# A differential-attention stage: the second map's weight moves from VectorE into PE's transposes, and row maxima are written negated

## The chip, the cores and the metric

The kernel runs on one core of a Trainium2 chip, in one launch. Its time is the device time of that core in microseconds (us); lower is better. The engines are PE (TensorE, matrix products), DVE (VectorE), ACT (ScalarE), POOL (GpSimd) and SP (SyncE, which here only issues DMAs). They run side by side and meet at semaphores; each works through its own instructions in order.

## The reference, cut to what matters

The reference is one step of a two-layer decoder over a prompt of 512 tokens and eight sample sequences of one new token each. Layer 1 is gated linear attention, layer 2 is differential attention with a linear position bias, and both end in a mixture of experts. Only differential attention bears on the change. For the prompt:

```python
bias = jnp.where(dist >= 0, -slopes[:, None, None] * dist, -jnp.inf)
p1 = jax.nn.softmax(jnp.einsum('bqhd,bkhd->bhqk', qf[..., :DH_B], k1) + bias, axis=-1)
p2 = jax.nn.softmax(jnp.einsum('bqhd,bkhd->bhqk', qf[..., DH_B:], k2) + bias, axis=-1)
return jnp.einsum('bhqk,bkhv->bqhv', p1 - lam * p2, vf)
```

There are 8 heads; queries come in 4 blocks of 128; causality lets block i see (i + 1) x 128 keys. For the samples, each of the 8 sequences attends with the same two-map rule over 2048 cached keys and values, kept in 16 pages of 128 positions (512 KB for keys and 512 KB for values, each), and its own new one.

## The kernel before, in words

The stage `stage_attention` does both jobs in one loop of eight passes. Pass b computes head b of the prompt and the scores of sample sequence b; the value products of sequence b-1 run in it too. Passes 0, 1 and 7 are written out, 2 to 6 are a loop on the chip. Every engine has its own order, written out by hand; there is no planner.

A pass has four blocks, i = 0 to 3 (a unit u = 4b + i is one query block of one head).

VectorE, in block i (`body` of the vector engine): the sums of key pages 4i and 4i+1 (`sum_page`, L2108: a reduce of a product of 128x1024 to 16 numbers per partition); `weigh` of the block before (L2065 to L2071); `keep` (L2075, the finished output of an earlier block out of PSUM); the sum of page 4i+2; `multiply` (L2098: key page 4i+4 by the query row); the sum of page 4i+3; and `unit` (bias onto the scores, L2084; row maxima, L2088; their sign, L2090). Behind block 3 come the sum of the new key's product, the softmax of the sample scores (L2140 to L2160) with `weigh` of block 3 inside it, and `fold`.

`weigh` makes lm = -lam * l1 / l2 from the two row sums l1 and l2 (ScalarE's exponentials accumulate them), and L2071 adds lm times the second map to the first, over (i + 1) x 128 columns. `keep` scales by 1 / l1 at the end.

GpSimd multiplies the three key pages in four that VectorE doesn't (L1894, 128x1024), into two buffers. Product n may start when the sum of product n-2 is done.

ScalarE, per unit: `c_copy` (L2017, the transposed map out of PSUM) for the block before, then the two exponentials (L2037) once VectorE has posted `nb_ok` at L2090. In a pass it also copies keys and queries of the next head, writes a finished sample row (`row_out`) and takes the exponential of the sample scores (L2048).

PE, in block i: the scores of the unit (L1976); values of pages 4i and 4i+1 of the sequence before (L1940); `finish` of the block before, that is the transposes of the weighed map (L1911, one per 128 columns, waiting for `c_ok` of L2071) and its product with the values (L1916); values of pages 4i+2 and 4i+3. Behind block 3: the small products of the sample softmax (L1959 to L1963), then `finish` of block 3.

SP issues the page loads: keys into a ring of eight page buffers, freed by the sums; values into a ring of four, freed by PE's value products; once a pass the query row of the sequence, broadcast to all partitions (L1866).

In `stage_queries`, which runs ahead, VectorE copies lam out of PSUM (L1746) into a column of `small`.

Of the kernel before, what the change touches and what calls it, by code (L numbers as in the profile page):

```python
# [9 lines left out]
ALU = mybir.AluOpType  # L10
ACT = mybir.ActivationFunctionType
AX = mybir.AxisListType


P = 128
D = 1024
# [1605 lines left out]
def stage_queries(nc, ctx, m, a, ahead):  # L1622

    sem = lambda n: ctx.enter_context(m_semaphore(nc, f"q_{n}"))
# [14 lines left out]
    m.pt = m.small[0:1, 128:128 + NS * PAGES].bitcast(I32)  # L1639
    t0, t1, pt_in = sem("t0"), sem("t1"), sem("pt_in")  # L1640
    m.coef = m.small[:, 33:34]
    sh_mm, sh_cp = sem("sh_mm"), sem("sh_cp")
    shares = m.R[:, 7168:7680]
    qs = m.R[0:NS, 5120:6144]
# [6 lines left out]
    with nc.Block() as block:  # L1651
# [75 lines left out]
        @block.vector  # L1727
        def _(v):
            v.wait_ge(t0, 3)
            for h in range(HB):  # L1730
                nc.vector.tensor_scalar(m.bt[:, 0:PAGES, 2 * h:2 * h + 2], nd.unsqueeze(2).to_broadcast([P, PAGES, 2]),
                                        2.0 ** (-8.0 * (h + 1) / HB), None, ALU.mult)
            for c in range(2):
                v.wait_ge(sh_mm, c + 1)
                wait(v, smm, c)
                nc.vector.tensor_copy(shares, m.ps[5][:, :]).then_inc(sh_cp, 1)
            v.wait_ge(l_in, 64)
            nc.vector.tensor_tensor(lprod, lrow[:, 0:2 * DHB], lrow[:, 2 * DHB:4 * DHB], ALU.mult)
            v.drain()
            nc.vector.tensor_reduce(out=lsum, in_=lprod.rearrange("p (a b) -> p a b", b=DHB), axis=AX.X, op=ALU.add).then_inc(l_sum, 1)  # L1740
            v.wait_ge(l_exp, 1)
            nc.vector.tensor_tensor(lam1, lsum[:, 0:1], lsum[:, 1:2], ALU.subtract)
            v.drain()
            nc.vector.tensor_scalar(lam1, lam1, LAM_INIT, None, ALU.add).then_inc(l_row, 1)
            v.wait_ge(l_mm, 1)
            nc.vector.tensor_copy(m.lam, m.ps[4][:, 0:1])  # L1746
            v.wait_ge(tab3, 1)
            nc.vector.tensor_reduce(out=odd1, in_=odd8, axis=AX.X, op=ALU.add)
            v.drain()

            nc.vector.tensor_tensor(m.coef, odd1, m.lam, ALU.mult)
            v.drain()
            nc.vector.tensor_tensor(m.coef, m.coef, odd1, ALU.add)
            v.drain()
            nc.vector.tensor_scalar(m.coef, m.coef, -1.0, 1.0, ALU.mult, ALU.add)


def stage_attention(nc, ctx, m, a):
# [6 lines left out]
    sem = lambda n: ctx.enter_context(m_semaphore(nc, f"at_{n}"))  # L1765
    kr_ok, k_tr, kt_ok, sc_mm, sb_ok, nb_ok, p_ok, c_ok, c_tr, c_cp, o_mm, o_ev = (sem(n) for n in
        ("kr_ok", "k_tr", "kt_ok", "sc_mm", "sb_ok", "nb_ok", "p_ok", "c_ok", "c_tr", "c_cp", "o_mm", "o_ev"))
# [3 lines left out]
    v_in = [sem(f"v_in{u}") for u in range(2)]  # L1771
    q_in, kn_in, vn_in, o_out, os_in, z_ok = (sem(n) for n in
        ("q_in", "kn_in", "vn_in", "o_out", "os_in", "z_ok"))
    dp_ok, pp_ok = sem("dp_ok"), sem("pp_ok")
    ks_ok, mx_ok, mx_tr, mr_ok, mb_mm, sh_ok, e_ok, l_ok, l_mm, l_ev, pv_mm, om_ok, or_mm, or_ev = (sem(n) for n in
        ("ks_ok", "mx_ok", "mx_tr", "mr_ok", "mb_mm", "sh_ok", "e_ok", "l_ok", "l_mm", "l_ev", "pv_mm", "om_ok",
         "or_mm", "or_ev"))
    NQ = SEQ // P
# [9 lines left out]
    mx = [m.small[:, 40 + 2 * u:42 + 2 * u] for u in range(2)]  # L1788
    ls = [m.small[:, 44 + 2 * u:46 + 2 * u] for u in range(2)]
    r1 = [m.small[:, 48 + i:49 + i] for i in range(NQ)]  # L1790
    lm = m.small[:, 52:53]

    kp = [m.W[:, u * D:(u + 1) * D] for u in range(4)] + [m.lnr[:, 0, :], m.lnr[:, 1, :],
                                                        m.kk[:, NTT - 1, :], m.vv[:, NTT - 1, :]]
    vp = [m.W[:, (4 + u) * D:(5 + u) * D] for u in range(4)]
    xtf = m.xt[:, :, :].rearrange("p k t -> p (k t)")
    qb, kn = xtf[:, 0:D], xtf[:, D:2 * D]

    v_prod, g_prod = xtf[:, 2 * D:3 * D], [xtf[:, 3 * D:4 * D], m.v[:, NTT - 1, :]]
# [25 lines left out]
    with nc.Block() as block:  # L1825
# [72 lines left out]
        def _(pe):  # L1898
# [6 lines left out]

            def finish(u, i, h):

                pe.wait_ge(c_ok, u + 1)
                wait(pe, c_cp, u)
                for j in range(i + 1):  # L1910
                    last = nc.tensor.transpose(CT_B[:, j * P:(j + 1) * P], SP[i % 2][0][:, j * P:(j + 1) * P], m.ident[:, :])  # L1911
                last.then_inc(c_tr, 1)
                pe.wait_ge(c_cp, u + 1)
                wait(pe, o_ev, u)
                for j in range(i + 1):
                    last = nc.tensor.matmul(O_B[:, (i % 2) * DVB:(i % 2 + 1) * DVB], ct[i % 2][:, j * P:(j + 1) * P],  # L1916
                                            m.vv[:, j, bass.ds(h * DVB, DVB)], start=(j == 0), stop=(j == i))
                last.then_inc(o_mm, 1)
# [80 lines left out]
        @block.scalar  # L1999
        def _(s):  # L2000
            def stage(h):

                wait(s, k_tr, h)
                nc.scalar.copy(khr, m.kk[:, 0:NQ, bass.ds(h * P, P)]).then_inc(kr_ok, 1)

            def q_copy(h):
                wait(s, sc_mm, NQ * h)
                nc.scalar.copy(qh, m.qt[:, bass.ds(h, 1), :].rearrange("p a t -> p (a t)"))

            def k_copy(h):  # L2010
                s.wait_ge(k_tr, h + 1)
                nc.scalar.copy(kth, KT_B[:, :]).then_inc(kt_ok, 1)

            def c_copy(u, i):
                s.wait_ge(c_tr, u + 1)
                wait(s, o_mm, u - 1)
                nc.scalar.copy(ct[i % 2][:, 0:(i + 1) * P], CT_B[:, 0:(i + 1) * P]).then_inc(c_cp, 1)  # L2017

            def row_out(b):
                s.wait_ge(or_mm, b + 1)  # L2020
                wait(s, o_out, 16 * b)
                for n in range(2):
                    last = nc.scalar.copy(orow[:, n * 512:(n + 1) * 512], SC_B[n][0:1, :])
                last.then_inc(or_ev, 1)
                s.wait_ge(or_ev, b + 1)
                s.dma_start(m.osD[bass.ds(b, 1), :], orow).then_inc(o_out, 16)

            def body(b):
                st = isinstance(b, int)
                for i in range(NQ):  # L2030
                    u = NQ * b + i
                    if i:
                        c_copy(u - 1, i - 1)
                    s.wait_ge(nb_ok, u + 1)
                    for j in range(2):
                        x = SP[i % 2][j][:, 0:(i + 1) * P]
                        last = nc.scalar.activation(x, x, ACT.Exp, bias=mx[i % 2][:, j:j + 1], accum_out=ls[i % 2][:, j:j + 1])  # L2037
                    last.then_inc(p_ok, 1)
                    if i == 1 and not (st and b == HB - 1):
                        stage(b + 1)  # L2040
                    if i == NQ - 1 and not (st and b == HB - 1):
                        q_copy(b + 1)
                        k_copy(b + 1)
                    if i == 1 and not (st and b < 2):
                        row_out(b - 2)
                s.wait_ge(sh_ok, b + 1)
                wait(s, pv_mm, VG * b)
                nc.scalar.activation(PR[:, :, 0:C], S, ACT.Exp).then_inc(e_ok, 1)  # L2048
                c_copy(NQ * b + NQ - 1, NQ - 1)
            s.wait_ge(z_ok, 2)  # L2050
            stage(0)
            q_copy(0)
            k_copy(0)
            seqs(s, body)
            row_out(NS - 2)
            row_out(NS - 1)

        @block.vector
        def _(v):
            V = nc.vector  # L2060
            def weigh(u, i):

                v.wait_ge(p_ok, u + 1)
                p1, p2 = (SP[i % 2][j][:, 0:(i + 1) * P] for j in range(2))
                V.reciprocal(r1[i], ls[i % 2][:, 1:2])  # L2065
                V.tensor_scalar(lm, ls[i % 2][:, 0:1], m.lam, -1.0, ALU.mult, ALU.mult)
                v.drain()
                V.tensor_tensor(lm, lm, r1[i], ALU.mult)
                v.drain()
                V.reciprocal(r1[i], ls[i % 2][:, 0:1])  # L2070
                V.scalar_tensor_tensor(out=p1, in0=p2, scalar=lm, in1=p1, op0=ALU.mult, op1=ALU.add).then_inc(c_ok, 1)  # L2071

            def keep(u, i, h):
                v.wait_ge(o_mm, u + 1)
# [3 lines left out]
            def unit(b, i):  # L2078
                st = isinstance(b, int)
                u, w = NQ * b + i, (i + 1) * P  # L2080
                v.wait_ge(sc_mm, u + 1)
                wait(v, c_tr, u - 1)
                for j in range(2):
                    V.scalar_tensor_tensor(out=SP[i % 2][j][:, 0:w], in0=m.dist[:, SEQ - w:SEQ], scalar=m.slope[:, bass.ds(b, 1)],  # L2084
                                           in1=SC_B[j][:, 0:w], op0=ALU.mult, op1=ALU.add).then_inc(sb_ok, 1)
                v.drain()
                for j in range(2):
                    V.tensor_reduce(out=mx[i % 2][:, j:j + 1], in_=SP[i % 2][j][:, 0:w], axis=AX.X, op=ALU.max)  # L2088
                v.drain()
                V.tensor_scalar(mx[i % 2], mx[i % 2], -1.0, None, ALU.mult).then_inc(nb_ok, 1)  # L2090

            def multiply(b, j):

# [138 lines left out]
```

## Time and profile before

| | us |
|---|---|
| median of 3 runs | 2310.33 (2310.22 to 2314.02) |
| the profiled execution | 2309.59 |
| its span, first to last instruction | 2307.8 |
| PE busy in the span | 1646.7 (71%) |
| DVE busy | 905.0 (39%) |
| POOL busy | 388.8 (17%) |
| ACT busy | 373.9 (16%) |
| mean granted TensorE clock | 0.824 of 2.4 GHz |

The attention stage runs from about 1211 to 1720 us of the span. The shares of the table are means over stages with quite different limits, so the stage is to be read by itself. A matmul is listed with PE and its weight load with PEld. A row of the timeline gives start, duration, engine, line, operation, output<-input with their shapes, a count where neighbours were merged and, in brackets, the engine's idle time before and what ended it. On DVE an instruction's record overlaps the next one's by some 0.1 us.

### The profile page before, as it was taken

To read this page: it belongs to the slowest core of one execution; us is meant where nothing else is said; L and a number is where in the kernel's file an instruction comes from. 1 tells how busy PE (TensorE), PEld (TensorE's weight loads), DVE (VectorE), ACT (ScalarE), POOL (GpSimd) and SP (SyncE) were. 2 spreads that over 40 slices of the span, in tenths; PEclk is the share of its full clock that TensorE was granted. 3 is DMA by queue.
4 is the path that set the end of the run, shared out by engine and by line. 5 is a ranking of instruction groups with operands and counts; after the bars stand their busy time and mean duration, and the time that the engine had idled before them with its cause. 6 is when DMAs were issued, how large, how long until landed. Compare 5 with 4: busy or idle time off the path is not lost. (4 is left out here: it accounts for less than half of the span.)

```text
span 2307.8 us, 21696 instructions
## 1 busy us (share of the span) xinstructions
PE 1646.7 (71%) x6774; PEld 689.3 (30%) x6775; DVE 905.0 (39%) x1432; ACT 373.9 (16%) x723; POOL 388.8 (17%) x279
## 2 busy tenths in 40 slices
PE   3999967682789996489792555555557649989970
PEld 1443334231333332044331122222213323333320
DVE  1000154745100000720208999999946430000007
ACT  0001121111221222210011111111112101222222
POOL 0000000010100000300105555545510100000004
PEclk7999976695899998689895677777788759999995
DMA  7562513406698997842306777778752258999973
GB/s 277 193 249 82 213 73 115 163 0 248 267 428 348 391 428 312 325 136 77 110 1 239 282 277 290 288 268 299 282 189 104 72 203 347 376 428 428 428 330 111
DMA packets 109276, 558.27 MB, mean 242 GB/s; under 512 B 13438, under 2 KB 22399, under 8 KB 87692
## 3 DMA queue, kind: packets, MB, share of 16 engines
q1 hardware_dynamic: 95306, 508.41, 56.4%
q0 software_dynamic: 7904, 28.45, 3.3%
q10 hardware_dynamic: 5992, 20.48, 2.2%
q8 instruction: 41, 0.67, 0.1%
q14 instruction: 33, 0.26, 0.0%
HBM read 517.16 MB, written 40.13 MB: 241 GB/s over the span
## 5 line engine op out<-in xcount | busy, mean ns | idle before, releaser
L1393 PE MATMUL ps<-arena_w,arena_r 128*64 128x512 f32 x1664 | 379.8, 613 | 32.4 <-issue 27.3
L1393 PEld LDWEIGHTS ps<-arena_w,arena_r 128*64 128x64 f32 x1664 | 129.1, 141 | 276.8 <-issue 268.4
L1375 PE MATMUL ps<-arena_w,arena_r 128*64 128x512 f32 x832 | 188.4, 601 | 19.2 <-ACT arena_r L1423 19.2
L1470 DVE TENSOR_TENSOR arena_r<-arena_r,ps 128x512 f32<-128x512 f32 x38 | 26.2, 688 | 441.4 <-ACT arena_r L1440 441.4
L1940 PE MATMUL ps<-arena_w,arena_r 128*32 128x512 f32 x504 | 142.4, 798 | 27.9 <-DMA arena_w<-in_cache_v_dram 27.9
L1894 POOL TENSOR_TENSOR xt<-arena_w,xt 128x1024 f32<-128x1024 f32 x48 | 120.6, 2513 | 166.4 <-DVE arena_w L2108 85.9
L433 PE MATMUL ps<-arena_w,xt 128*128 128x512 f32 x256 | 113.5, 600 | 0.4 <-PE ps L206 0.4
L927 PE MATMUL ps<-arena_w,xt 128*128 128x512 f32 x256 | 111.1, 593 | 0.0
L1595 PE MATMUL ps<-arena_w,xt 128*128 128x512 f32 x256 | 110.9, 594 | 0.0
L2108 DVE TENSOR_REDUCE arena_w<-xt 128x16 f32<-128x1024 f32 x88 | 105.2, 1210 | 1.4 <-POOL xt L1894 1.2
L335 PE MATMUL ps<-ident,arena_r 128*128 128x128 f32 (+1 forms) x200 | 42.4, 377 | 86.7 <-DVE arena_r L326 86.7
L1325 POOL COPY small<-idx 128x1 int32 (+1 forms) x38 | 6.9, 182 | 569.0 <-PE ps L1341 487.3
L1463 DVE COPY arena_r<-ps 128x512 f32<-128x512 f32 x38 | 26.3, 691 | 194.0 <-PE ps L1375 194.0
L996 POOL TENSOR_TENSOR x_res<-x_res,arena_m 128x1024 f32<-128x1024 f32 (+1 forms) x20 | 52.6, 2630 | 289.8 <-DVE x_res L990 289.8
L1375 PEld LDWEIGHTS ps<-arena_w,arena_r 128*64 128x64 f32 x832 | 57.1, 138 | 124.3 <-issue 102.6
L1894 POOL TENSOR_TENSOR arena_w<-arena_w,xt 128x1024 f32<-128x1024 f32 x32 | 75.8, 2370 | 38.0 <-DVE arena_w L2108 38.0
L1439 ACT ACTIVATE arena_r<-ps 64x512 f32<-64x512 f32 x38 | 22.4, 588 | 360.3 <-PE ps L1393 360.3
L401 PE MATMUL ps<-xt,arena_w 128*128 128x512 f32 x128 | 72.1, 656 | 0.9 <-PEq L293 0.6
L1976 PE MATMUL ps<-arena_r 64*128 64x128 f32 (+3 forms) x128 | 32.7, 595 | 56.0 <-DVE arena_r L2084 39.3
L2037 ACT ACTIVATE arena_r<-arena_r,small 128x128 f32<-128x128 f32 (+3 forms) x64 | 35.4, 554 | 227.8 <-DVE small L2090 227.8
L433 PEld LDWEIGHTS ps<-arena_w,xt 128*128 128x128 f32 x256 | 48.3, 192 | 66.6 <-issue 66.6
L1595 PEld LDWEIGHTS ps<-arena_w,xt 128*128 128x128 f32 x256 | 48.4, 190 | 63.4 <-issue 63.4
(319 smaller groups left out, 2222.8 us busy)
## 6 DMA issues: line engine op xcount, KB each, us to landing
arena_w<-in_w_exp_gate_dram SPq DMA_DIRECT2D x38, 2048.0 KB, 12.5
arena_w<-in_w_exp_up_dram SPq DMA_DIRECT2D x38, 2048.0 KB, 18.8
arena_w<-in_w_exp_down_dram SPq DMA_DIRECT2D x38, 2048.0 KB, 17.7
arena_w<-in_cache_v_dram SPq DMA_DIRECT2D x126, 512.0 KB, 5.1
arena_w<-in_cache_k_dram SPq DMA_DIRECT2D x96, 512.0 KB, 4.8
arena_w<-in_w_ada_dram SPq DMA_DIRECT2D x12, 2048.0 KB, 14.9
arena_m<-in_w_ada_dram SPq DMA_DIRECT2D x12, 2048.0 KB, 10.7
y_rows<-arena_r ACTq DMA_DIRECT2D x38, 512.0 KB, 10.7
```

What stands on the lines that cost most here:

```text
L335: last = nc.tensor.transpose(m.ps[4 * (i % 2) + k // 4][:, (k % 4) * P:(k % 4) * P + r], xm[i % 2][0:r, :].rearrange("t (p k) -> t k p", k ...
L401: nc.tensor.matmul(m.ps[n % 2][:, :], w, m.xt[:, k, 0:SEQ], start=(k == 0), stop=(k == KT - 1))
L433: last = nc.tensor.matmul(m.ps[4 + n % 4][:, :], m.xt[:, k, i * P:(i + 1) * P], m.wr[c % 2][:, k, :], start=(k == 0), stop=(k == KT - 1))
L927: last = nc.tensor.matmul(m.ps[(4 if n % 2 else 6) + c][0:r, :], m.xt[:, k, i * P:i * P + r], w[:, k, c * 512:(c + 1) * 512], start=(k == ...
L996: nc.gpsimd.tensor_tensor(m.x[0:r, i, :], m.x[0:r, i, :], m.lnr[0:r, 1, :], ALU.add).then_inc(self.done, 1)
L1375: last = nc.tensor.matmul(psy[c][at:at + 64, :], ht[u][:, k, 64 * (1 - a):64 * (2 - a)], wd[u][:, k, c * 512:(c + 1) * 512], start=(k == 0 ...
L1393: last = nc.tensor.matmul(ps[at:at + 64, :], xgt[u][:, k, 64 * a:64 * (a + 1)], w[u][:, k, :], start=(k == 0), stop=(k == KT - 1), tile_po ...
L1595: last = nc.tensor.matmul(m.ps[4 + n % 4][:, :], m.xt[:, k, i * P:(i + 1) * P], m.wr[c % 2][:, k, :], start=(k == 0), stop=(k == KT - 1))
L1894: G.tensor_tensor(g_prod[n % 2], kp[j % RING], qb, ALU.mult).then_inc(pp_ok, 1)
L1940: last = nc.tensor.matmul(PSO[n][g * CP:(g + 1) * CP, :], PR[:, j, :], bufs[j % 2][:, c], start=(j < GRP), stop=(j >= PAGES - GRP and g > ...
L2037: last = nc.scalar.activation(x, x, ACT.Exp, bias=mx[i % 2][:, j:j + 1], accum_out=ls[i % 2][:, j:j + 1])
L2108: V.tensor_reduce(out=S[:, j, :], in_=prod.rearrange("p (c d) -> p c d", d=DHB), axis=AX.X, op=ALU.add).then_inc(ks_ok, 1)
```

## The change

The second map is no longer added to the first on VectorE. For each block of 128 columns PE now runs two matmuls into the same PSUM block: the first map against the identity, and the second map against a diagonal matrix that holds lm. PE's accumulation makes transpose(p1 + lm * p2) of it. ScalarE writes the diagonal matrix (128x128) from the identity with lm as its scale, into one of two buffers in free columns of `xt`, and posts `dl_ok`, for which PE now waits. VectorE posts `c_ok`, for which ScalarE waits, as soon as lm is there; lm has two columns, one for even and one for odd blocks, and is made by one instruction from l1, 1 / l2 and a column that holds -lam. The row maxima are written negated by the reduce itself.

```diff
@@ stage_queries, vector engine
             nc.vector.tensor_copy(m.lam, m.ps[4][:, 0:1])
+            nc.vector.tensor_scalar(m.neg_lam, m.ps[4][:, 0:1], -1.0, None, ALU.mult)
@@ stage_attention
-    lm = m.small[:, 52:53]
+    lm = [m.small[:, 52 + i:53 + i] for i in range(2)]
+    dl = [xtf[:, 4 * D + u * P:4 * D + (u + 1) * P] for u in range(2)]
@@ PE, finish
-                pe.wait_ge(c_ok, u + 1)
+                pe.wait_ge(dl_ok, u + 1)
                 wait(pe, c_cp, u)
                 for j in range(i + 1):
-                    last = nc.tensor.transpose(CT_B[:, j * P:(j + 1) * P], SP[i % 2][0][:, j * P:(j + 1) * P], m.ident[:, :])
+                    block = slice(j * P, (j + 1) * P)
+                    nc.tensor.matmul(CT_B[:, block], SP[i % 2][0][:, block], m.ident[:, :], start=True, stop=False)
+                    last = nc.tensor.matmul(CT_B[:, block], SP[i % 2][1][:, block], dl[i % 2], start=False, stop=True)
@@ ScalarE
+            def second_weight(u, i):
+                s.wait_ge(c_ok, u + 1)
+                nc.scalar.activation(dl[i % 2], m.ident[:, :], ACT.Copy, scale=lm[i % 2]).then_inc(dl_ok, 1)
...
                     if i:
+                        second_weight(u - 1, i - 1)
                         c_copy(u - 1, i - 1)
...
+                second_weight(NQ * b + NQ - 1, NQ - 1)
                 s.wait_ge(sh_ok, b + 1)
@@ VectorE, weigh
                 v.wait_ge(p_ok, u + 1)
-                p1, p2 = (SP[i % 2][j][:, 0:(i + 1) * P] for j in range(2))
                 V.reciprocal(r1[i], ls[i % 2][:, 1:2])
-                V.tensor_scalar(lm, ls[i % 2][:, 0:1], m.lam, -1.0, ALU.mult, ALU.mult)
                 v.drain()
-                V.tensor_tensor(lm, lm, r1[i], ALU.mult)
+                V.tensor_scalar(lm[i % 2], ls[i % 2][:, 0:1], r1[i], m.neg_lam, ALU.mult, ALU.mult).then_inc(c_ok, 1)
                 v.drain()
                 V.reciprocal(r1[i], ls[i % 2][:, 0:1])
-                V.scalar_tensor_tensor(out=p1, in0=p2, scalar=lm, in1=p1, op0=ALU.mult, op1=ALU.add).then_inc(c_ok, 1)
@@ VectorE, unit
                 for j in range(2):
-                    V.tensor_reduce(out=mx[i % 2][:, j:j + 1], in_=SP[i % 2][j][:, 0:w], axis=AX.X, op=ALU.max)
-                v.drain()
-                V.tensor_scalar(mx[i % 2], mx[i % 2], -1.0, None, ALU.mult).then_inc(nb_ok, 1)
+                    last = V.tensor_reduce(out=mx[i % 2][:, j:j + 1], in_=SP[i % 2][j][:, 0:w], axis=AX.X, op=ALU.max, negate=True)
+                last.then_inc(nb_ok, 1)
```

## Rows read from the trace of the kernel before

**Rows 1.** Window over the stage: us, busy time (instructions), clock, DMA share, GB/s.

```profile
1211.00:1720.00 509.00, 268.25 (x1016) 102.76 (x1017) 452.31 (x623) 74.38 (x206) 248.87 (x98) 0.71 0.74 272
```

**Rows 2.** Waits, 1300 to 1600 us: total us, times, longest.

```profile
ACT arena_r L2037 <- DVE small L2090: 136.9, 20, 11.3
...
PEld ps L1940 <- DMA arena_w<-in_cache_v_dram: 27.1, 15, 4.3
```

**Rows 3.** Timeline of DVE, end of block 0 and its weights, fourth pass.

```profile
1410.35 0.48 DVE L2088 TENSOR_REDUCE small<-arena_r 128x1 f32<-128x128 f32 x2
1410.91 2.23 DVE L2090 TENSOR_SCALAR small<-small 128x2 f32<-128x2 f32 x1
1413.06 1.21 DVE L2108 TENSOR_REDUCE arena_w<-xt 128x16 f32<-128x1024 f32 x1
...
1415.31 0.15 DVE L2065 RECIPROCAL small<-small 128x1 f32<-128x1 f32 x1
1415.38 0.19 DVE L2066 TENSOR_SCALAR small<-small 128x1 f32<-128x1 f32 x1
1415.64 2.18 DVE L2068 TENSOR_TENSOR small<-small 128x1 f32<-128x1 f32 x1
...
1417.98 0.33 DVE L2071 SCALAR_TENSOR_TENSOR arena_r<-arena_r,small 128x128 f32<-128x128 f32 x1
1418.23 0.35 DVE L2075 TENSOR_SCALAR arena_w<-ps,small 128x128 f32 x1
```

**Rows 4.** Timeline of POOL over the same time and the next block.

```profile
1410.78 2.33 POOL L1894 TENSOR_TENSOR xt<-arena_w,xt 128x1024 f32<-128x1024 f32 x1
1415.47 2.35 POOL L1894 TENSOR_TENSOR arena_w<-arena_w,xt 128x1024 f32<-128x1024 f32 x1 [2.35 <-DVE arena_w L2108]
1419.78 3.26 POOL L1894 TENSOR_TENSOR xt<-arena_w,xt 128x1024 f32<-128x1024 f32 x1 [1.97 <-DVE arena_w L2108]
```

**Rows 5.** Timeline of DVE: L2090 of blocks 1, 2 and 3, and a reduce.

```profile
1420.75 1.21 DVE L2108 TENSOR_REDUCE arena_w<-arena_w 128x16 f32<-128x1024 f32 x1
...
1423.66 1.72 DVE L2090 TENSOR_SCALAR small<-small 128x2 f32<-128x2 f32 x1
...
1436.55 1.20 DVE L2090 TENSOR_SCALAR small<-small 128x2 f32<-128x2 f32 x1
...
1449.59 0.17 DVE L2090 TENSOR_SCALAR small<-small 128x2 f32<-128x2 f32 x1
```

**Rows 6.** DVE groups by form, 1240 to 1700 us: busy us, mean ns, idle before.

```profile
L2147 DVE TENSOR_SCALAR arena_w<-ident,arena_w 16x16 f32<-16x16 f32 x8 | 12.3, 1533 | 0.6
L2071 DVE SCALAR_TENSOR_TENSOR arena_r<-arena_r,small 128x512 f32<-128x512 f32 x8 | 12.0, 1503 | 0.0
...
L2071 DVE SCALAR_TENSOR_TENSOR arena_r<-arena_r,small 128x384 f32<-128x384 f32 x8 | 4.8, 599 | 0.0
...
L2071 DVE SCALAR_TENSOR_TENSOR arena_r<-arena_r,small 128x256 f32<-128x256 f32 x8 | 3.7, 466 | 0.0
```

**Rows 7.** Timeline of all engines, end of the third pass.

```profile
1392.81 0.15 DVE L2065 RECIPROCAL small<-small 128x1 f32<-128x1 f32 x1
...
1393.84 2.55 POOL L1894 TENSOR_TENSOR xt<-arena_w,xt 128x1024 f32<-128x1024 f32 x1 [10.67 <-DMA xt<-q_sample_rows]
...
1394.46 1.96 DVE L2147 TENSOR_SCALAR arena_w<-ident,arena_w 16x16 f32<-16x16 f32 x1
...
1401.49 1.23 DVE L2098 TENSOR_TENSOR xt<-arena_w,xt 128x1024 f32<-128x1024 f32 x1 [0.77 <-issue]
```

**Rows 8.** Groups of PE and of ACT by form, 1240 to 1700 us.

```profile
L1911 PE MATMUL ps<-ident,arena_r 128*128 128x128 f32 x79 | 22.0, 399 | 43.6 <-DVE arena_r L2071 43.6
...
L2017 ACT COPY arena_r<-ps 128x128 f32<-128x128 f32 x8 | 2.1, 265 | 38.4 <-PE ps L1911 38.4
```

**Rows 9.** Timeline of PE at the fourth pass's end.

```profile
1452.19 0.38 PE L1959 MATMUL ps<-ident,arena_w 128*16 128x128 f32 x1 [3.35 <-DVE arena_w L2142]
```

**Rows 10.** Window of the busiest DMA stretch; columns as in rows 1.

```profile
1499.00:1511.00 12.00, 7.24 (x29) 2.71 (x25) 11.69 (x17) 1.79 (x5) 2.39 (x2) 0.72 1.00 380
```

More of the change, by code:

```diff
@@ L1641, in stage_queries @@
     m.coef = m.small[:, 33:34]
+    m.neg_lam = m.small[:, 34:35]
     sh_mm, sh_cp = sem("sh_mm"), sem("sh_cp")
@@ L1773, in stage_attention @@
         ("q_in", "kn_in", "vn_in", "o_out", "os_in", "z_ok"))
-    dp_ok, pp_ok = sem("dp_ok"), sem("pp_ok")
+    dp_ok, pp_ok, dl_ok = sem("dp_ok"), sem("pp_ok"), sem("dl_ok")
     ks_ok, mx_ok, mx_tr, mr_ok, mb_mm, sh_ok, e_ok, l_ok, l_mm, l_ev, pv_mm, om_ok, or_mm, or_ev = (sem(n) for n in
```

## The prediction

> **What bounds the kernel now.** The chain that ended last covers only the final normalisation, so I read the stage the diff touches by itself. The window over attention (1211 to 1720 us) has VectorE busy 452 of 509 us, PE 268, GpSimd 249, ScalarE 74, DMA at 272 GB/s [rows 1]. The waits of its middle say the same: ScalarE waits longest for L2090 on VectorE, PE's longest wait for a transfer is 27 us in 300, and VectorE waits for nothing long [rows 2]. So a microsecond is worth what VectorE's own row of instructions gives back, eight times over (8 passes of the body, about 60 us each).
>
> VectorE is busy, but not with work. L2090 changes the sign of two numbers per partition and takes 2.23 us; L2068 multiplies one number and takes 2.18 us [rows 3]. GpSimd's page products explain both: L2090 ends at 1413.14, GpSimd's product at 1413.11; L2068 ends at 1417.82, the product at 1417.81 [rows 4]. Some VectorE instructions stand until GpSimd's ends, and the other way round: the product of 1419.78 takes 3.26 us in place of 2.33, because a VectorE product had started just before. A reduce is not held: L2108 at 1420.75 takes its 1.21 us inside that product [rows 4, 5]. Where GpSimd is idle L2090 takes 0.17 us [rows 5].
>
> **The change part by part.**
>
> *L2090 and its drain go.* The reduces write the negated maximum themselves; I take a negating reduce at the price of a plain one. L2090 starts 0.08 us behind the second reduce and the next instruction starts 0.09 before it ends, where it would start 0.08 before the reduce's end. So a unit gains L2090's duration plus 0.07: 2.30, 1.79, 1.27 and 0.24 us for i = 0 to 3 [rows 3, 5], 5.6 us a pass, 45 us in all. This holds if what follows isn't held in its turn. Two reduces follow (pages 4i+4 and 4i+5). The second needs the product of page 4i+5, which ended before L2090 did (1410.81 for i = 0 [rows 4]), and its end then falls at about 1413.1, just as GpSimd comes free at 1413.11 to begin the next product. So GpSimd can follow for i = 0 with nothing to spare, for i = 1 and 2 with some.
>
> *L2071 goes from VectorE.* From its start to the next instruction's: 0.25 us for i = 0, and duration less 0.09 for i = 1 and 2: 0.38 and 0.51 [rows 3, 6]. 1.14 a pass, 9 us in all.
>
> *L2066 and L2068 become one TENSOR_SCALAR with two scalars read from SBUF.* L2065 starts 0.16 us before GpSimd's product; L2066, 0.07 later, still slips in ahead of it; L2068 comes 0.17 behind its start and stands [rows 3, 4]. The new instruction needs L2065's result, so it starts behind a drain, at L2065 + 0.23: 0.07 us too late. If a one-column TENSOR_SCALAR is held as the two-column L2090 and the 16-column L2147 are [rows 3, 6], it ends with the product, where L2068 ended, and the swap gains nothing in i = 0 to 2. Its ends: 0, or about 1.7 us each if it isn't held (below). I take 0, by L2090, the nearest instruction in kind.
>
> *The last block of a pass (i = 3).* Here GpSimd waits for the next query row, which lands about 6 us after page 15's sum. From L2065 to the next pass's first product a calm pass takes 8.68 us (1392.81 to 1401.49) [rows 7]: 0.73 for L2071, 1.96 for L2147, 5.99 for the rest. Over the seven passes with a successor L2071 averages (12.0 - 0.7)/7 = 1.6 and L2147 (12.3 - 0.2)/7 = 1.7 [rows 6], so 9.3. After it, L2071 is gone and L2147 starts about 0.9 behind L2065. Either it is held to the end of the first product, or it passes and the copy L2156, 3 us on, is held to the end of the second. Both give 7.5 to 8.3; I take 8.0: 1.3 x 7 = 9 us, and 0.7 in the last pass.
>
> *PE and ScalarE.* Each of the ten blocks of a pass gets one matmul more, 0.40 us at the clock of this stage: 4.0 us a pass. ScalarE gets a 128x128 activation per unit, and PE waits for it in place of VectorE: 0.27 us and a hand-over, say 0.4 [rows 8]. What hides them is PE's waiting for VectorE. The tightest place is the pass's end: PE has done its values and waits 3.35 us for the row maxima [rows 9]. Three matmuls (1.2) and the hop (0.4) leave about 1.7. Without that cover they cost up to 5.6 us a pass. Queued behind the hop are the value matmuls 2i+1 and the next scores; these are wanted a whole block later. At the stage's end nothing hides the last unit: 4 x 0.40, the hop left out since the transposes wait behind L1963 already: 1.6 us. The added column in the query stage is 0.1.
>
> *Sum:* 45 + 9 + 9 + 0.7 - 1.7 = 62 us. The profiled execution took 2309.6 us (span 2307.8), 0.7 under the median of 2310.3, so I predict 2247.5.
>
> **A rule against the trace.** That L2068 and L2147 stand with GpSimd is in the rows above. The Trainium skill (SBUF — State Buffer, "Who interferes with whom") gives two grounds for it: two inputs in SBUF, as L2068, or a two-port mode, as a TENSOR_SCALAR may enter. VectorE: DVE Perf Modes ("Mode 2×_2P") lets an instruction enter that mode where its outermost dimension that isn't 1 is even, or odd and equal on both sides; an operand of one column has no such dimension. The change thus swaps an instruction that surely takes the lock for one where the rule is silent. By the one reading the sum stays, by the other the rival below holds. No row shows a one-column TENSOR_SCALAR inside a product: L2066 always gets in first.
>
> **The rivals.**
>
> *The new TENSOR_SCALAR is not held.* Then weigh ends about 2 us earlier, the reduce of page 4i+2 runs beside the product, and the multiply that follows is held instead, to the product's end at L2065 + 2.5: it needs 1.0 more, so the next reduce starts at 3.5. Held, the weights end at 2.6, and keep, a reduce and a multiply (0.3 + 1.13 + 1.13) bring it to 5.2. That is 1.7 x 24 = 41 us more: 2206. But a pass moves 33 transfers of 512 KB (16 key pages, 16 value pages, the query broadcast), 17.3 MB; in 47 us that is 369 GB/s, against 380 in the busiest stretch [rows 10]. So part is lost: 2206 to 2225, I say 2214. For: the silent rule, one column. Against: two columns are held.
>
> *DMA holds the pass back.* In the forecast a pass takes about 52 us, 333 GB/s, but a block with eight pages 10.3 us: 407 GB/s, over the 380 seen. At 380 the block takes 11.0; 0.7 x 24 = 17 us lost: 2264. For: the share of 1.00 there. Against: the key ring is eight pages deep and transfers pause at each pass's end, so the lag can be made up.
>
> *Slower: PE's order becomes the bound.* If the extra matmuls and the hop come out behind the value pages that PE waits for, the 3.35 us go and the rest is VectorE's wait for scores and maxima. It decides once PE's row of a pass grows by over 3.4 us at that place; with nothing covered it is 5.6 x 8 = 45 us and the gains vanish: 2355. Against: PE is busy 268 of 509 us.
>
> *It gives nothing:* the time of L2090 only moves to the next instruction that stands with GpSimd, or to a wait for its products, and the stage keeps its pace: about 2305.
>
> **How the numbers follow.** Forecast 0.50 (own range 2240 to 2256), not held 0.22, DMA 0.18, slower 0.06, nothing 0.04. The range 2208 to 2266 leaves out part of the second, and the last two. Under 0.2% (4.6 us) a measurement can't tell from no change: faster 0.90, same 0.04, slower 0.06.
>
> **What would show it.** VectorE: nothing between the reduces and L2108; the new TENSOR_SCALAR near 2.2 us for i = 0 to 2 (0.2 if the first rival holds); passes of 52 us. GpSimd's gap before the product of page 4i+7 down from 2.35 us [rows 4] to under 0.7. PE's wait before L1959 near 1.7 us. Wrong, if VectorE shows waits for PE or DMA, if the negating reduce takes longer than 0.24 us at 128 columns, or if passes stay near 60 us.

## The result and the profile after

| | before | changed |
|---|---|---|
| median of the runs | 2310.27 us (4 runs, 2310.13 to 2314.02) | 2234.05 us (4 runs, 2222.03 to 2240.12) |
| ratio to before, with its 95% interval | | 0.9663 [0.9643, 0.9682] |
| the profiled execution, its span | 2309.6, 2307.8 us | 2240.12, 2238.4 us |
| mean pass of the attention body (7 passes, first product to first product on VectorE) | 60.3 us | 50.6 us |

The changed kernel is 76 us faster; the forecast was 63 us faster. The gain is where it was looked for. From the copy of lam (L1746 before, L1747 after) to the first instruction of the next stage (L870), VectorE's rows count 515.5 us before and 440.1 us after, 75.4 us less. The stages ahead of it grew by 1.6 us and those behind it by 4.4, and the profiled execution, at 69.5 us under that of before, is the slowest of its four.

First the windows over the stage and over the busiest 12 us of transfers, as in [rows 1, 10]. The columns are the length in us, then busy us and number of instructions of PE, PE's weight loads, VectorE, ScalarE and GpSimd, then the granted clock, the DMA share and GB/s:

```profile
1211.00:1650.00 439.00, 289.35 (x1258) 139.44 (x1258) 342.33 (x529) 89.08 (x242) 253.36 (x98) 0.76 0.85 316
1399.00:1411.00 12.00, 10.85 (x56) 4.61 (x57) 10.08 (x16) 2.38 (x7) 5.37 (x3) 1.00 1.01 394
```

VectorE was busy 89% of the stage and is busy 78%: 452 us have become 342, which is 110 us less work or standing, for 75 us less time. GpSimd's busy time is what it was (249, 253). PE has 242 instructions more; 240 of them are three more for each of the 80 blocks of 128 columns, where the forecast counted one (below). The transfers' share rose from 0.74 to 0.85. So VectorE gave back more than the stage did, and the waits say what it now waits for. The same 300 us as in [rows 2], of the changed kernel:

```profile
ACT arena_r L2022 <- PE ps L1916: 113.8, 23, 6.6
...
PE ps L1945 <- DMA arena_w<-in_cache_v_dram: 33.1, 22, 2.7
...
DVE arena_w L2152 <- PE ps L1964: 14.0, 6, 4.2
...
DVE arena_r L2092 <- PE ps L1981: 8.0, 5, 2.0
...
DVE small L2075 <- ACT arena_r L2047: 4.0, 6, 0.9
```

ScalarE's 137 us of waiting for L2090 are gone. VectorE now waits 14.0 us for PE's transposed row maxima (L2152), 8.0 us for scores (L2092) and 4.0 us for the exponentials, and PE itself waits for value pages from memory.

VectorE's row around block 0 of the fourth pass, the place of [rows 3], shows how the pass lost its 10 us:

```profile
1382.72 0.48 DVE L2096 TENSOR_REDUCE small<-arena_r 128x1 f32<-128x128 f32 x2
1383.12 1.21 DVE L2115 TENSOR_REDUCE arena_w<-xt 128x16 f32<-128x1024 f32 x1
1384.24 1.21 DVE L2115 TENSOR_REDUCE arena_w<-arena_w 128x16 f32<-128x1024 f32 x1
1385.37 0.15 DVE L2075 RECIPROCAL small<-small 128x1 f32<-128x1 f32 x1
1385.61 0.27 DVE L2077 TENSOR_SCALAR small<-small 128x1 f32<-128x1 f32 x1
1385.97 0.16 DVE L2079 RECIPROCAL small<-small 128x1 f32<-128x1 f32 x1
1386.15 0.35 DVE L2083 TENSOR_SCALAR arena_w<-ps,small 128x128 f32 x1
1386.42 1.21 DVE L2115 TENSOR_REDUCE arena_w<-xt 128x16 f32<-128x1024 f32 x1
1387.54 1.43 DVE L2105 TENSOR_TENSOR xt<-arena_w,xt 128x1024 f32<-128x1024 f32 x1
...
1405.31 0.27 DVE L2077 TENSOR_SCALAR small<-small 128x1 f32<-128x1 f32 x1
```

And GpSimd's row over the same time and a later block, the place of [rows 4]:

```profile
1383.15 2.35 POOL L1897 TENSOR_TENSOR xt<-arena_w,xt 128x1024 f32<-128x1024 f32 x1
1385.53 2.36 POOL L1897 TENSOR_TENSOR arena_w<-arena_w,xt 128x1024 f32<-128x1024 f32 x1
1387.84 3.34 POOL L1897 TENSOR_TENSOR xt<-arena_w,xt 128x1024 f32<-128x1024 f32 x1
...
1404.52 2.36 POOL L1897 TENSOR_TENSOR arena_w<-arena_w,xt 128x1024 f32<-128x1024 f32 x1 [2.51 <-DVE arena_w L2115]
```

Three things are to be seen. Nothing stands between the maxima and the next reduce (1382.72, 1383.12), where L2090 took 2.23 us. GpSimd's product of page 7 follows that of page 6 after 0.03 us (1385.53), where it had a gap of 2.35. And L2077 at 1405.31 takes 0.27 us in the middle of a product that runs from 1404.52 to 1406.88: it is not held, where L2068 stood for 2.18 us. The multiply that comes next is the one that shares the time (1387.54, 1.43 us).

The groups by form over 1230 to 1630 us (busy, mean ns of one | idle before), of the changed kernel:

```profile
L2077 DVE TENSOR_SCALAR small<-small 128x1 f32<-128x1 f32 x32 | 8.7, 273 | 2.5
L2096 DVE TENSOR_REDUCE small<-arena_r 128x1 f32<-128x128 f32 x16 | 3.8, 281 | 0.8
L1915 PE MATMUL ps<-ident,arena_r 128*128 128x128 f32 x160 | 45.7, 379 | 5.0 <-ACT xt L2026 5.0
L1916 PE MATMUL ps<-xt,arena_r 128*128 128x128 f32 x160 | 41.1, 350 | 0.0
L2026 ACT ACTIVATE xt<-ident,small 128x128 f32<-128x128 f32 x32 | 12.9, 402 | 27.8 <-DVE small L2077 25.2 <-ACT arena_m L2032 2.6
```

All 32 fused instructions take about 0.27 us, and 24 of them begin inside a product of GpSimd's.

The 80 blocks show 160 records at L1915 and 160 at L1916, where L1911 had one a block [rows 8]: a matmul of this kind (fp32) is recorded as two instructions, a transpose as one. PE's row for the four blocks of the last unit, before:

```profile
1698.99 1.09 PE L1911 MATMUL ps<-ident,arena_r 128*128 128x128 f32 x4
```

The first of the four in the changed kernel:

```profile
1621.80 0.78 PE L1915 MATMUL ps<-ident,arena_r 128*128 128x128 f32 x2
1622.36 0.64 PE L1916 MATMUL ps<-xt,arena_r 128*128 128x128 f32 x2
```

The four take 1.09 us before and 3.76 after (1621.80 to 1625.56). Over the whole stage the stretches of these instructions add up to 22.4 us before and 62.9 after, 5.1 us more a pass.

### The profile page after: what moved, and what is told of

Read it like the earlier page. It is cut to its first block and busy times, and to the rows that moved or that the text cites. A ratio compares the mean times of both kernels' runs of the same rounds, so it can differ in the third digit from the quotient of the medians.

```text
span 2238.4 us, 22081 instructions
## 1 busy us (share of the span) xinstructions
PE 1670.7 (75%) x7014; PEld 724.6 (32%) x7015; DVE 794.9 (36%) x1337; ACT 386.3 (17%) x755; POOL 393.3 (18%) x279
## 5 line engine op out<-in xcount | busy, mean ns | idle before, releaser
L1945 PE MATMUL ps<-arena_w,arena_r 128*32 128x512 f32 x504 | 129.4, 729 | 43.1 <-DMA arena_w<-in_cache_v_dram 43.1
L2115 DVE TENSOR_REDUCE arena_w<-xt 128x16 f32<-128x1024 f32 x88 | 105.5, 1210 | 5.4 <-POOL xt L1897 5.1
L1439 ACT ACTIVATE arena_r<-ps 64x512 f32<-64x512 f32 x38 | 22.4, 590 | 364.5 <-PE ps L1393 364.5
L433 PEld LDWEIGHTS ps<-arena_w,xt 128*128 128x128 f32 x256 | 48.2, 191 | 66.6 <-issue 66.6
L1595 PEld LDWEIGHTS ps<-arena_w,xt 128*128 128x128 f32 x256 | 48.7, 192 | 63.9 <-issue 63.9
L927 PEld LDWEIGHTS ps<-arena_w,xt 128*128 128x128 f32 x256 | 48.2, 190 | 60.0 <-issue 58.4
L335 PEld LDWEIGHTS ps<-ident,arena_r 128*128 128x128 f32 (+1 forms) x200 | 34.8, 213 | 98.9 <-DVE arena_r L326 98.9
```

The lines of the kernel that those rows point to most:

```text
L335: last = nc.tensor.transpose(m.ps[4 * (i % 2) + k // 4][:, (k % 4) * P:(k % 4) * P + r], xm[i % 2][0:r, :].rearrange("t (p k) -> t k p", k ...
L433: last = nc.tensor.matmul(m.ps[4 + n % 4][:, :], m.xt[:, k, i * P:(i + 1) * P], m.wr[c % 2][:, k, :], start=(k == 0), stop=(k == KT - 1))
L927: last = nc.tensor.matmul(m.ps[(4 if n % 2 else 6) + c][0:r, :], m.xt[:, k, i * P:i * P + r], w[:, k, c * 512:(c + 1) * 512], start=(k == ...
L1595: last = nc.tensor.matmul(m.ps[4 + n % 4][:, :], m.xt[:, k, i * P:(i + 1) * P], m.wr[c % 2][:, k, :], start=(k == 0), stop=(k == KT - 1))
L1945: last = nc.tensor.matmul(PSO[n][g * CP:(g + 1) * CP, :], PR[:, j, :], bufs[j % 2][:, c], start=(j < GRP), stop=(j >= PAGES - GRP and g > ...
L2115: V.tensor_reduce(out=S[:, j, :], in_=prod.rearrange("p (c d) -> p c d", d=DHB), axis=AX.X, op=ALU.add).then_inc(ks_ok, 1)
```

## The experiments

Three questions: what each part of the change is worth, whether the one-column TENSOR_SCALAR is what puts the time under the forecast of 2247.5 us, and what stops the pass at 50.6 us.

**Repeat, and the parts.** The changed kernel as it is:

> The changed kernel as it is, again, as the yardstick for the runs beside it on this chip: 2222 to 2240 us, passes of 50 to 52 us, VectorE waiting some 26 us of the stage for PE's scores (L2092), PE's transposed maxima (L2152) and the exponentials (L2075).

Measured: 2231.62 us (2227.35 to 2241.64), ratio 0.966 [0.9622, 0.9698]; passes of 50.61 us. The executions of this kernel spread over 0.6 to 0.8%, so a comparison with it is good to some 5 us.

The first part alone, on the kernel before; then the changed kernel with L2090 put back:

```diff
 (before)
-                    V.tensor_reduce(out=mx[i % 2][:, j:j + 1], ..., op=ALU.max)
-                v.drain()
-                V.tensor_scalar(mx[i % 2], mx[i % 2], -1.0, None, ALU.mult).then_inc(nb_ok, 1)
+                    last = V.tensor_reduce(out=mx[i % 2][:, j:j + 1], ..., op=ALU.max, negate=True)
+                last.then_inc(nb_ok, 1)
 (changed: the same lines the other way round)
```

> The kernel before with one part of the change: the reduces write the negated maxima, L2090 and its drain are gone; the weights stay as they were. Theory (sizes of the prediction): 5.6 us a pass, 45 us in all, 2265 us; L2068 still takes 2.2 us. Rival (the time of L2090 moves to the next held instruction or to a wait for GpSimd's products): 2290 us or more.

> The changed kernel with L2090 and its drain put back. In the changed kernel VectorE waits some 26 us of the stage for PE's scores and maxima and for the exponentials. Theory (those waits are PE's and the transfers' own pace, so what VectorE loses is in part hidden by them): 2255 to 2270 us, and VectorE's waits for PE shrink. Rival (VectorE's row still sets everything, the parts add up): 45 us more than the changed kernel, 2279 us, the waits unchanged.

Measured: e1 2263.03 us, ratio 0.9808 [0.9783, 0.9833]; that is 45.6 us under the 2308.6 that the kernel before took beside it, with passes of 54.74 us. e2: 2257.14 us, 0.9772 [0.9748, 0.9796], passes of 53.19. So the first part alone is worth 46 us, the rest alone 51 us, and both together 76 to 80: some 20 us are lost where they meet. In e2 VectorE's waits for scores are gone again and those for the transposed maxima are down to 1.6 us in the same 300.

**Is the fused instruction free of GpSimd, and what is that worth?** Four kernels, all from the changed one. In the first two the same result comes from an instruction over two or three columns; in the third from a one-column product of two tensors; the fourth brings the subtraction back to VectorE behind the fused instruction, with no extra matmuls and no diagonal matrix.

```diff
 e3
+                V.tensor_scalar(lm2[i % 2], ls[i % 2][:, 0:2], r1[i], m.neg_lam, ALU.mult, ALU.mult).then_inc(c_ok, 1)
 e9 (a third column in ls, set to 1.0 once)
+                V.tensor_scalar(lm3[i % 2], ls[i % 2][:, 0:3], r1[i], m.neg_lam, ALU.mult, ALU.mult).then_inc(c_ok, 1)
 e4
+                V.tensor_scalar(lm[i % 2], ls[i % 2][:, 0:1], m.neg_lam, None, ALU.mult)
+                v.drain()
+                V.tensor_tensor(lm[i % 2], lm[i % 2], r1[i], ALU.mult).then_inc(c_ok, 1)
 e5
+                V.scalar_tensor_tensor(out=p1, in0=p2, scalar=lm[i % 2], in1=p1, op0=ALU.mult, op1=ALU.add).then_inc(c_ok, 1)
```

> The changed kernel with one edit: the instruction that makes lm works on two columns (both row sums) in place of one; the second is not used. Theory (a TENSOR_SCALAR stands while GpSimd multiplies if its columns are even in number, and doesn't with one column): it takes about 2.2 us in blocks 0 to 2, VectorE's waits for PE shrink, 2245 to 2260 us. Rival (what frees it is its form, two scalars read from SBUF, or its place): 0.27 us and the changed kernel's 2234 us.

> The changed kernel with lm's instruction on three columns (the two row sums and a constant; the last two results unused). Theory (what frees one column is that there is nothing to split in two halves; three columns, odd and equal on both sides, are split): it stands with GpSimd, 2.2 us in blocks 0 to 2, 2245 to 2260 us. Rival (an odd number of columns frees it): 0.3 us and 2222 to 2240 us.

> The changed kernel with lm made in two steps as before: a one-column TENSOR_SCALAR by -lam, a drain, and a one-column TENSOR_TENSOR by 1 / l2. This is the state that the prediction assumed (the weight's instruction held to the end of GpSimd's product). Theory (the fused form is worth up to 1.7 us in each of 24 blocks, less what PE and transfers hold back): the TENSOR_TENSOR takes 2.2 us and the time is the predicted 2247 us. Rival (the fusing is worth nothing, the rest of the gain came from elsewhere): 2234 us.

> The changed kernel with the second map added on VectorE again: negated maxima and the fused one-column instruction stay, the diagonal, ScalarE's step and the second matmul go, PE waits for VectorE's addition. Theory (the addition reads two tensors in SBUF and stands with GpSimd's product, so it inherits the hold that the fused instruction escapes): the addition takes 2.3 us or more in blocks 0 to 2, and the time is that of the negated maxima alone, 2258 to 2264 us. Rival (the fused instruction is worth its 20 us without the move to PE): 2243 us.

| | us | ratio | mean pass |
|---|---|---|---|
| e3, two columns | 2254.20 | 0.9752 [0.972, 0.9784] | 52.99 |
| e9, three columns | 2254.76 | 0.9764 [0.9745, 0.9784] | 53.43 |
| e4, product of two tensors | 2255.11 | 0.9775 [0.9748, 0.9802] | 52.70 |
| e5, subtraction on VectorE | 2256.95 | 0.9779 [0.9763, 0.9795] | 53.61 |

The instruction's group by form over 1230 to 1600 us (busy, mean ns of one | idle before), of e3:

```profile
L2078 DVE TENSOR_SCALAR small<-small 128x2 f32<-128x2 f32 x28 | 50.6, 1808 | 2.2
```

The same group of e9:

```profile
L2081 DVE TENSOR_SCALAR small<-small 128x3 f32<-128x3 f32 x28 | 52.8, 1885 | 2.2
```

Of e4:

```profile
L2078 DVE TENSOR_TENSOR small<-small 128x1 f32<-128x1 f32 x29 | 51.0, 1757 | 2.2
```

And of e5, the subtraction at two widths and the fused instruction (L2073 there):

```profile
L2077 DVE SCALAR_TENSOR_TENSOR arena_r<-arena_r,small 128x384 f32<-128x384 f32 x7 | 15.6, 2230 | 0.2 <-issue 0.2
L2077 DVE SCALAR_TENSOR_TENSOR arena_r<-arena_r,small 128x128 f32<-128x128 f32 x7 | 14.1, 2012 | 0.0
L2073 DVE TENSOR_SCALAR small<-small 128x1 f32<-128x1 f32 x28 | 7.6, 273 | 2.2
```

One column more is the whole difference between 273 ns and 1808. It is the shape that decides, and the four kernels in which something on that path stands with GpSimd lie within 3 us of each other, 20 to 25 us above the changed one. In e5 the fused instruction itself still takes 273 ns; the subtraction behind it stands instead, at 2.0 to 2.2 us where it took 0.33 to 0.60 in the kernel before [rows 3, 6]. So moving the subtraction off VectorE is what keeps the gain of the fused instruction: either part without the other gives little more than e1.

**What holds the pass at 50.6 us?** Four kernels, again from the changed one. One matmul per block in place of two (the second map is left out of the result; diagonal and wait stay, and so does the first matmul, two records where the transpose was one); half of each value page loaded (the other half of the values is stale); the maxima's transposes ahead of the last value products, with the sample's fold behind; and half pages together with e4's two instructions.

```diff
 e6
-                    nc.tensor.matmul(CT_B[:, block], SP[i % 2][0][:, block], m.ident[:, :], start=True, stop=False)
-                    last = nc.tensor.matmul(CT_B[:, block], SP[i % 2][1][:, block], dl[i % 2], start=False, stop=True)
+                    last = nc.tensor.matmul(CT_B[:, block], SP[i % 2][0][:, block], m.ident[:, :], start=True, stop=True)
 e7
-                    sp.dma_start(buf, vs[bass.ds(page, 1)].rearrange("g p n -> p (g n)")).then_inc(loaded, 16)
+                    sp.dma_start(buf[:, 0:512], vs[bass.ds(page, 1)].rearrange("g p n -> p (g n)")[:, 0:512]).then_inc(loaded, 16)
 e8
+                    if i == NQ - 1:
+                        maxima(b)        # before the last value products, where softmax(b) had it behind them
 (and fold(b - 1) on VectorE moved from before the sample's row sums to behind them, with a drain)
 e10 = e4 and e7
```

> The changed kernel without the second matmul of each block: PE transposes the first map alone, so the second map is left out of the prompt's result; ScalarE still writes the diagonal and PE still waits for it. PE has ten matmuls fewer a pass, 4 us at 0.40 us each. Theory (PE's order now sets the end of a pass: its scores and maxima come late): VectorE's waits at L2092 and L2152 shrink by more than half, 2212 to 2226 us. Rival (PE is late because the value pages are, so it would only wait longer for them): within 4 us of the changed kernel.

> The changed kernel with half of each value page loaded (the first 512 columns; the rest of the buffer keeps old data, so the samples' values are not the reference's): 13.1 MB a pass in place of 17.3. Theory (the transfers hold PE back: value pages land late behind the key pages, and the query row too): PE's waits for value pages, GpSimd's for the query row and VectorE's at L2152 shrink, 2205 to 2220 us. Rival (PE's own instructions are what is late): within 6 us of the changed kernel.

> The changed kernel with PE's order altered at the end of a pass: the transposed maxima and their broadcast (L1964, L1966) come ahead of the last value products, and VectorE folds the sequence before only behind the row sums. Theory (VectorE waits 2 to 3 us a pass there because those value products, late by their pages, stand ahead in PE's queue): the wait at L2152 goes, and since the sample's exponential still has to wait for those value products about 1.2 us a pass are left, 8 us: 2226 us. Rival (the value products end later by as much and the next pass starts no sooner): 2234 us, no change.

> The run with half of each value page loaded and, as before the change, a TENSOR_SCALAR and a TENSOR_TENSOR for lm (the samples' values are again not the reference's). With whole pages the fused form was worth 20 us. Theory (1.7 us in each of 24 blocks, of which the transfers take back half when whole pages are loaded): with the transfers relieved the difference to the half-page run with the fused form is 35 to 41 us, 2248 to 2254 us. Rival (the fused form is worth 20 us by itself, the 1.7 us is wrong): 2233 us.

| | us | ratio | mean pass |
|---|---|---|---|
| changed | 2231.62 to 2234.05 | 0.966 | 50.6 |
| e6, one matmul | 2230.48 | 0.9643 [0.9615, 0.9672] | 49.96 |
| e8, maxima first | 2238.99 | 0.968 [0.9644, 0.9717] | 50.43 |
| e7, half value pages | 2212.55 | 0.9574 [0.9547, 0.96] | 47.29 |
| e10, half pages, held instruction | 2252.14 | 0.9749 [0.9733, 0.9765] | 53.04 |

e6 is not distinguishable from the changed kernel: the second map's matmuls, two of the three records that a block has more, cost next to nothing. The third was not taken out. e7 takes 19 us off, measured on the same chip as the repeat. Its waits over 1300 to 1600 us:

```profile
PE ps L1945 <- DMA arena_w<-in_cache_v_dram: 14.3, 15, 2.0
...
DVE xt L2105 <- DMA xt<-q_sample_rows: 6.8, 5, 2.1
...
DVE arena_w L2115 <- POOL arena_w L1897: 5.5, 5, 1.1
DVE arena_w L2115 <- POOL xt L1897: 5.0, 5, 1.0
...
DVE arena_w L2152 <- PE ps L1964: 0.3, 1, 0.3
DVE arena_r L2092 <- PE ps L1981: 0.2, 1, 0.2
```

VectorE's 14.0 and 8.0 us of waiting for PE have become 0.3 and 0.2, with the same PE instructions in the same order. What made VectorE wait was PE's waiting for value pages, passed on. The window over those 300 us, of the changed kernel:

```profile
1300.00:1600.00 300.00, 210.71 (x912) 98.50 (x908) 247.76 (x382) 62.04 (x172) 182.96 (x70) 0.78 0.89 337
```

and of e7:

```profile
1300.00:1600.00 300.00, 210.49 (x991) 101.56 (x992) 263.63 (x412) 68.54 (x186) 191.45 (x73) 0.84 0.80 267
```

VectorE is busy 88% of it, against 83% in the changed kernel (and 94% in the kernel before, 282 of the same 300 us). What it still waits for is mostly the next query row (6.8 us) and GpSimd's products (10.5 us). The granted clock is higher too, 0.84 against 0.78, but that alone does not do it: e8 has 0.85 over the same 300 us and passes of 50.43 us. Half value pages lighten all transfers (337 to 267 GB/s); the runs do not separate the value pages' own lateness from that.

e10 says the rest: where the instruction is held, half pages bring next to nothing (52.70 us a pass with whole ones, 53.04 with halves; 0.9775 and 0.9749 as ratios, 6 us at most). By ratios e10 lies 40 us above e7 (0.0175 x 2310), and e4 lies 27 us above the changed kernel (0.0115 x 2310; 21 to 23.5 by the medians, which were not taken side by side). An instruction that isn't held is thus worth 40 us with light transfers, and whole value pages take back 13 to 19 of them.

In e8 the order was changed where VectorE waits longest, and nothing was gained: its median is 7 us higher, with overlapping intervals. Its waits:

```profile
PE ps L1945 <- DMA arena_w<-in_cache_v_dram: 23.8, 15, 3.0
...
DVE arena_w L2163 <- ACT arena_r L2063: 19.1, 6, 3.5
```

The wait for the maxima is gone, and a wait of 3.2 us a pass for the sample's exponential stands in its place: that one waits for PE's value products (L1950), which wait for the same pages. The order of PE's work decides where the lag shows, not how long it is. None of the kernels above that compute the whole result beats the changed one.

## Why the prediction was right, and which step of it failed

**L2090 and its drain go (forecast 45 us): right.** e1 gives 45.6. What the forecast named is in the rows: the reduce takes 281 ns at 128 columns in both kernels, plain or negating (0.48 us for the two, [rows 3]), and GpSimd's product of page 4i+7 follows at once, with "nothing to spare" for i = 0: 1385.50 to 1385.53.

**L2066 and L2068 become one (forecast 0): this step failed.** "If a one-column TENSOR_SCALAR is held as the two-column L2090 and the 16-column L2147 are" had the right condition and the wrong answer, "I take 0, by L2090, the nearest instruction in kind". It passes GpSimd's product in all 24 blocks in which it meets one. The rows of before had no such case: L2066 always came ahead of the product. The rival had it, with its price: 1.7 x 24 = 41 us. e10 against e7 puts it at 40, as far as transfers allow. The Trainium skill (VectorE: DVE Perf Modes, "Mode 2×_2P") asks for an outermost dimension other than 1 that is even, or odd and equal on both sides; e9's three columns stand, which agrees with the odd case, and for one column, on which the rule is silent, the runs show that the instruction does not wait for GpSimd's product.

**The rival's limit by transfers: right in kind, and smaller than measured.** The forecast let the not-held case lose up to 19 us to transfers (2206 to 2225) and took 8. Measured are 2232 to 2234, 26 to 28 over 2206: 13 to 19 us are lost to the value pages (e7, e10), and 7.6 is what the sum falls short by in its own case already (e4, below); up to a few us stay without a name. The time thus lies between the two ranges that were given for the forecast (2240 to 2256) and for this rival, in neither of them. The 380 GB/s of [rows 10] was no ceiling: the changed kernel moves 394 GB/s in its busiest 12 us. The rival "DMA holds the pass back" named the right cause, but for a pass of 52 us, and there, as e4 and e10 show, whole pages cost 6 us at most, against 17 forecast. Each of the two rivals held half of what happened: the instruction passes, and then the pages decide.

**L2071 and the last block (forecast 9 + 9 us).** e4 is the forecast's own case, with the multiply that makes lm held. Its passes take 52.7 us against "52" in the forecast. Its time of 2255.1 is 7.6 over 2247.5, and 53.5 under the kernel before, where the sum said 62. Its profiled execution (2252.0, the fastest of its four) is 57.6 us under that of before. Seven passes gave 52.9 there in place of 8.04 x 7 = 56.3, the last pass with what follows it in the stage 5.0 in place of 5.8, the stages ahead took 3.7 us less and those behind 4.1 more. So the terms for a pass were well sized, 0.5 us too high. The 1.6 us for the last unit, which "nothing hides", were too few: its four blocks take 2.7 us more in the changed kernel. And of the stages behind no term was made at all: they took 1.7 to 4.4 us more in two profiled executions of the changed kernel. What lengthens those was not tried.

**PE and ScalarE (forecast: hidden, 1.7 us left before L1959): hidden, as far as tried; left, no.** ScalarE's step takes the 0.40 us that it was given with its hand-over. PE's price was too low: "Each of the ten blocks of a pass gets one matmul more, 0.40 us", but each block has gone from one record to four, since a transpose is one and these matmuls are two each. The finishes take 5.1 us more a pass in place of 4.0; for the three blocks ahead of the maxima it is 1.06 us (0.55 to 1.61), under the 1.2 forecast, and for the four behind them 2.7. That this is covered is e6's result for the second map's half: without those ten matmuls a pass nothing changes. But PE's slack of 3.35 us [rows 9] is spent. PE's row at the fourth pass's end, of the changed kernel:

```profile
1412.20 0.94 PE L1921 MATMUL ps<-arena_w,arena_r 128*128 x6 [0.57 <-ACT arena_r L2022]
1415.30 0.62 PE L1945 MATMUL ps<-arena_w,arena_r 128*32 128x512 f32 x2 [2.16 <-DMA arena_w<-in_cache_v_dram]
...
1418.10 0.38 PE L1964 MATMUL ps<-ident,arena_w 128*16 128x128 f32 x1
```

PE comes late to the maxima by its wait for a page, and VectorE stands 3.24 us for them. The forecast counted three matmuls and a hop against that slack; it did not count that a pass of 50 us asks for its pages in 10 us less. "Slower: PE's order becomes the bound" saw the place, not the cause.

**The signs.** Two of the forecast's signs came: nothing stands between the reduces and L2115, and GpSimd's gap went from 2.35 us to 0.03. The fused instruction (0.27 us) and the pass (50.6) went the first rival's way. Of the three signs of being wrong, "VectorE shows waits for PE or DMA" did come, with 22 us of 300 for PE. The limit of 0.24 us for the negating reduce says nothing: it is half of a pair of overlapping records, and the plain reduce of before takes 0.28 as well.

**The size.** By the runs: 46 (L2090) + 8 (subtraction off VectorE with lm's multiply still held, e1 to e4) + 21 to 27 (lm's multiply not held) = 75 to 81, against 76 to 80 measured. The forecast's 62 was 8 too high in its own case and left out the third term, of which transfers then took back a part. That the time falls within the whole range of 2208 to 2266 is in part luck: these errors partly cancel.

## What to carry to other kernels

When an engine looks busy, compare the length of its smallest instructions with the work in them: here two instructions on one or two numbers per partition took 2.2 us each, and their ends fell on the ends of another engine's products. To make such an instruction pass, change its form (one tensor input, one column) or fold it into one that passes (the negation in the reduce), and check that the next instruction of the other kind isn't the one to stand now, as e5's did. Then rework the transfer rate at the new length of a pass: what a faster engine gives back is cut at the pages it asks for sooner.

## What was not expected of the hardware

- A TENSOR_SCALAR with two scalar operands over 128x1 fp32 takes 0.27 us inside a GpSimd product (in all 24 cases); over 128x2 and 128x3 it takes 1.81 and 1.89 us in the mean. A TENSOR_TENSOR over 128x1 stands like the wide ones (1.76 us in the mean). That is as the Trainium skill (SBUF — State Buffer, "Who interferes with whom") has it, with two inputs in SBUF, and this case shows that it holds down to a single column.
- A VectorE product that waits for GpSimd's to end goes ahead of GpSimd's next one, which is queued without a gap: 1387.54 with 1.43 us, then 1387.84 with 3.34 in place of 2.35. So the two engines' products take turns here.
- The changed kernel's executions spread by 0.8 and 0.6% in its two sets, those of before by 0.2 to 0.5% in its four, and those of e7, with half pages, by 0.2%. That fits a pass that now waits for transfers, and isn't shown beyond that.
